# Attention value sums: the base block chosen for each half of the key rows, the rest of the window as 256-column products

## The reference

```python
q = apply_rope(...).reshape(B, nblk, WINDOW, KV_HEADS, Q_PER_KV, HEAD_DIM)   # 16 blocks of 128 queries
logits = jnp.einsum("bnqkgd,bnskd->bnkgqs", q, k_band)                       # 256 keys: block before, own block
valid = (diff >= 0) & (diff < WINDOW)                                        # diff = 128 + query - key
probs = softmax(concat([masked logits, sink]))[..., :-1]
o = jnp.einsum("bnkgqs,bnskd->bnqkgd", probs, v_band)
```

## Time and profile before

| | |
|---|---|
| median of three runs | 2229.74 us |
| span of the profiled execution | 2230.9 us |
| TensorE busy | 2163.5 us (97%) |
| VectorE, ScalarE, GpSimd busy | 64%, 46%, 46% |
| DMA share by slices | 44% to 99% |

### The profile page before, as it was taken

How to read it: one execution, slowest core, us unless ns; L and a number is a source line. 1 busy time by engine, 2 the same in 40 slices (tenths; PEclk the granted TensorE clock), 3 DMA queues, 4 the chain that set the end, 5 groups by cost and what they waited for, 6 DMA issues and landing times.

```text
span 2230.9 us, 28791 instructions
## 1 busy us (share of the span) xinstructions
PE 2163.5 (97%) x10410; PEld 1808.6 (81%) x10410; DVE 1436.8 (64%) x1815; ACT 1032.7 (46%) x1898; POOL 1037.3 (46%) x636
## 2 busy tenths in 40 slices
PE   5999999999999999999999999999999999999998
PEld 4887778788888878888787888887888888888887
DVE  6966548757476864554974653867676657657764
ACT  4334445634545644445644445434444434434442
POOL 2556775845553865544684555440222232232222
PEclk9999999999999999999999999999999999999999
DMA  9888899785559795557876565989677797787554
GB/s 344 307 300 309 310 319 343 236 309 174 201 189 334 277 322 173 197 192 279 312 277 247 179 211 206 353 341 361 226 282 243 260 342 251 268 313 274 196 203 170
DMA packets 244782, 592.86 MB, mean 266 GB/s; under 512 B 20928, under 2 KB 96800, under 8 KB 244256
## 3 DMA queue, kind: packets, MB, share of 16 engines
q1 hardware_dynamic: 241680, 585.71, 72.8%
q10 hardware_dynamic: 2960, 5.30, 0.7%
HBM read 461.96 MB, written 119.54 MB: 261 GB/s over the span
## 4 chain that ended last, share of the span: by engine, by line
PE 74%; DMA 7%; POOL 6%; DVE 5%; ACT 3%; DVEq 2%; POOLq 1%; issue 1%; SPq 1%; ACTq 0%
PE ps L2272 22%; PE ps L2274 22%; PE ps L2273 22%; POOL w_lo L1110 3%; DMA w_raw<-in_a_w_in 2%; PE ps L2477 2%; POOL cbl L1129 1%; PE ps L2527 1%; PE ps L2526 1%; PE ps L2552 1%; DMA zo<-tt 1%; DVE yb L2018 1%; DMA w_raw<-a_weights_combined 1%; DMA r<-b_input 1%; ACT w_hi L1304 1%
## 5 line engine op out<-in xcount | busy, mean ns | idle before, releaser
L1110 POOL TENSOR_TENSOR w_lo<-w_raw,w_hi 128x1024 fp32r<-128x1024 f32 x244 | 650.4, 2684 | 568.8 <-ACT w_hi L1304 568.8
L1304 ACT ACTIVATE w_hi<-w_raw 128x1024 fp32r<-128x1024 f32 x260 | 271.7, 1057 | 413.8 <-DMA w_raw<-in_a_w_in 370.2
L2272 PE MATMUL ps<-h,w_hi 128*128 128x512 f32 x1024 | 403.2, 394 | 10.2 <-POOL w_lo L1110 9.4
L2274 PE MATMUL ps<-h,w_lo 128*128 128x512 f32 x1024 | 398.9, 390 | 0.0
L2273 PE MATMUL ps<-h,w_hi 128*128 128x512 f32 x1024 | 398.7, 389 | 0.0
L1249 POOL TENSOR_SCALAR_AFFINE_SELECT pt<-pt 128x512 fp32r<-128x512 f32 x128 | 82.2, 642 | 395.4 <-ACT pt L1666 338.9
L2272 PEld LDWEIGHTS ps<-h,w_hi 128*128 128x128 f32 x1024 | 192.2, 188 | 55.5 <-POOL w_lo L1110 14.7
L2274 PEld LDWEIGHTS ps<-h,w_lo 128*128 128x128 f32 x1024 | 192.2, 188 | 40.6
L2273 PEld LDWEIGHTS ps<-h,w_hi 128*128 128x128 f32 x1024 | 192.4, 188 | 38.9 <-issue 0.2
L2272 PE MATMUL ps<-r,w_hi 128*128 128x512 f32 x480 | 191.7, 399 | 3.8 <-ACT kvf L1608 2.3
L2274 PE MATMUL ps<-r,w_lo 128*128 128x512 f32 x480 | 187.7, 391 | 0.0
(11 more groups left out here) (268 smaller groups left out, 4636.8 us busy)
## 6 DMA issues: line engine op xcount, KB each, us to landing
w_raw<-in_a_w_in SPq DMA_DIRECT2D x256, 256.0 KB, 3.6
w_hi<-b_weights_split SPq DMA_DIRECT2D x104, 512.0 KB, 4.4
w_lo<-b_weights_split SPq DMA_DIRECT2D x104, 512.0 KB, 5.8
w_raw<-in_a_w_in SPq DMA_DIRECT2D x52, 512.0 KB, 4.9
w_raw<-in_a_w_out SPq DMA_DIRECT2D x48, 512.0 KB, 5.7
w_hi<-v_weights_combined SPq DMA_DIRECT2D x48, 512.0 KB, 4.0
w_lo<-v_weights_combined SPq DMA_DIRECT2D x48, 512.0 KB, 5.1
w_hi<-a_weights_combined SPq DMA_DIRECT2D x32, 512.0 KB, 6.3
```

The costliest lines, as they stand in the source:

```text
L1110: g.tensor_tensor(wlo[p][:, rows_], raw[p][:, rows_], whi[p][:, rows_].bitcast(F32), ALU.subtract).then_inc(w_lo, 1)
L1304: s_.activation(whi[p][:, rows_], raw[p][:, rows_], ACT.Copy).then_inc(w_hi, 1)
L2272: t_.matmul(dst_, stat[0], mov[0], start=start, stop=False)
L2274: return t_.matmul(dst_, stat[1], mov[0], start=False, stop=stop)
```

## The change

The base block is chosen for each half of the key rows. Rows 0 to 63 take V of the own block, rows 64 to 127 take V of the block before (`vst` keeps no fifth block for that). What is then wrong are two corners: key rows 0 to 63 for queries 0 to 63 above the diagonal, and key rows 64 to 127 for queries 64 to 127 under it. Elsewhere a query half needs no correction in one half of the rows. So 64 rows are free in each correction, and the rest part of the probabilities is put there: one tile `pe_` of 128 rows holds the rounded part in one half and the rest in the other, with the difference of V (`edge_low`, `edge_up`) stored in both halves of the rows. Two corrections of 512 columns become two of 256.

With this go:

- TensorE: `values` issues two matmuls of 512 columns and two of 256, with separate waits ahead of them.
- VectorE: after L2234 two more subtractions of 64x256 that write the rests of the corners, before `pt_lo` is raised; L2234 itself raises the new `pt_all`. `kv_rest` has seven instructions for three, `kv_shift` two subtractions for one, and loses a copy.
- ScalarE: `kv_round` has seven instructions for three. The wait for `xk_out[1]` and `hb_out[1]` moves from the first write to `pt` to the first write to `pp`, since `pp` now lies on `hbs1`.
- GpSimd: `mask` has four selections of 64x256 for two of 128x512, a drain and a wait at its end.
- Some tiles move (`ot`, `obt`, the third `wh`), and `keep` with its two prologue instructions goes.

```diff
@@ places
-        pt = place("pt", v_at + 16 * K, [4, 512], F32R)
-        pp = place("pp", v_at + 24 * K, [2, 4, P + 1], F32)
+        pt = place("pt", v_at + 16 * K, [2, 512], F32R)
+        pp = place("pp", v_at + 20 * K, [2, 4, P + 1], F32)
+        edge_low = place("edge_low", v_at + 24 * K + 64, [NC, KVH, P], F32R)
+        pe_ = place("p_edge", v_at + 28 * K + 64, [2, 4 * HEAD], F32R)
@@ GpSimd, mask
-                for m, ready in ((0, pt_hi), (1, pt_lo)):
-                    pool.wait_ge(ready, a + 1)
-                    last = g.affine_select(out=pt[:, 2 + m].rearrange("p (h q) -> p h q", h=4),
...
+                pool.drain()
+                pool.wait_ge(pt_hi, a + 1)
+                kept(pe_[64:P, 1], high[64:P, :, HEAD:P], True)
+                kept(pe_[0:64, 0], high[0:64, :, 0:HEAD], False)
+                pool.wait_ge(pt_lo, a + 1)
+                kept(pe_[0:64, 1], pe_[0:64, 1].rearrange("p (h q) -> p h q", h=4), True)
+                kept(pe_[64:P, 0], pe_[64:P, 0].rearrange("p (h q) -> p h q", h=4), False).then_inc(pt_masked, 1)
+                pool.wait_ge(pt_masked, a + 1)
@@ ScalarE, kv_round
-                s_.activation(vst[:, 1:5, kh, 0:HEAD], kvf[:, 1:5, cols_], ACT.Copy)
-                s_.activation(dst[:, :, kh, 0:HEAD], df[:], ACT.Copy).then_inc(kv_hi_done, 1)
+                s_.activation(vst[0:64, :, kh, 0:HEAD], kvf[0:64, 1:5, cols_], ACT.Copy)
+                s_.activation(vst[64:P, :, kh, 0:HEAD], kvf[64:P, 0:4, cols_], ACT.Copy)
+                for there in (slice(0, 64), slice(64, P)):
+                    s_.activation(edge_low[there, :, kh, 0:HEAD], df[0:64], ACT.Copy)
+                    last = s_.activation(edge_up[there, :, kh, 0:HEAD], df[64:P], ACT.Copy)
+                last.then_inc(kv_hi_done, 1)
@@ ScalarE, attention steps
                     if a >= 2:
                         act.wait_ge(pv_full, a - 1)
-                    else:
-                        act.wait_ge(xk_out[1], 16 * 2)
-                        act.wait_ge(hb_out[1], 16 * 2)
                     s_.activation(pt[:, 0, :], bank(6), ACT.Copy).then_inc(pt_hi, 1)
                 if 0 <= a < ATT:
                     act.wait_ge(m_ready, a + 1)
                     if a >= 2:
                         act.wait_ge(pt_full, a - 1)
+                    elif a == 0:
+                        act.wait_ge(xk_out[1], 16 * 2)
+                        act.wait_ge(hb_out[1], 16 * 2)
@@ VectorE, kv_rest
-                v.tensor_tensor(vst[:, 1:5, kh, HEAD:P], kvf[:, 1:5, cols_], vst[:, 1:5, kh, 0:HEAD].bitcast(F32),
-                                ALU.subtract)
-                v.tensor_tensor(dst[:, :, kh, HEAD:P], df[:], dst[:, :, kh, 0:HEAD].bitcast(F32), ALU.subtract) \
-                    .then_inc(kv_lo_done, 1)
+                v.tensor_tensor(vst[0:64, :, kh, HEAD:P], kvf[0:64, 1:5, cols_], vst[0:64, :, kh, 0:HEAD].bitcast(F32),
+                                ALU.subtract)
+                v.tensor_tensor(vst[64:P, :, kh, HEAD:P], kvf[64:P, 0:4, cols_], vst[64:P, :, kh, 0:HEAD].bitcast(F32),
+                                ALU.subtract)
+                for there in (slice(0, 64), slice(64, P)):
+                    v.tensor_tensor(edge_low[there, :, kh, HEAD:P], df[0:64], edge_low[0:64, :, kh, 0:HEAD].bitcast(F32),
+                                    ALU.subtract)
+                    last = v.tensor_tensor(edge_up[there, :, kh, HEAD:P], df[64:P],
+                                           edge_up[64:P, :, kh, 0:HEAD].bitcast(F32), ALU.subtract)
+                last.then_inc(kv_lo_done, 1)
@@ VectorE, attention steps
-                    v.tensor_tensor(pt[:, 1, :], bank(6), pt[:, 0, :].bitcast(F32), ALU.subtract).then_inc(pt_lo, 1)
+                    v.tensor_tensor(pt[:, 1, :], bank(6), pt[:, 0, :].bitcast(F32), ALU.subtract).then_inc(pt_all, 1)
...
+                    v.tensor_tensor(pe_[64:P, 0].rearrange("p (h q) -> p h q", h=4), turned_p[0:64, :, 0:HEAD],
+                                    high[0:64, :, 0:HEAD], ALU.subtract)
+                    v.tensor_tensor(pe_[0:64, 1].rearrange("p (h q) -> p h q", h=4), turned_p[64:P, :, HEAD:P],
+                                    high[64:P, :, HEAD:P], ALU.subtract).then_inc(pt_lo, 1)
@@ TensorE, values
                 pe.wait_ge(kv_lo_done, at("kv_lo_done", g, kh + 1))
-                pe.wait_ge(pt_masked, a + 1)
                 if a >= 1:
                     pe.wait_ge(o_done, a)
+                pe.wait_ge(pt_hi, a + 1)
                 t_.matmul(bank(7), vst[:, blk, kh, :], pt[:, 0, :], start=True, stop=False)
+                pe.wait_ge(pt_all, a + 1)
                 t_.matmul(bank(7), vst[:, blk, kh, :], pt[:, 1, :], start=False, stop=False)
-                t_.matmul(bank(7), dst[:, blk, kh, :], pt[:, 2, :], start=False, stop=False)
-                t_.matmul(bank(7), dst[:, blk, kh, :], pt[:, 3, :], start=False, stop=True).then_inc(pv_full, 1)
+                pe.wait_ge(pt_masked, a + 1)
+                by_query = bank(7).rearrange("p (h q) -> p h q", h=4)
+                t_.matmul(by_query[:, :, 0:HEAD], edge_low[:, blk, kh, :], pe_[:, 0, :], start=False, stop=False)
+                t_.matmul(by_query[:, :, HEAD:P], edge_up[:, blk, kh, :], pe_[:, 1, :], start=False, stop=True) \
+                    .then_inc(pv_full, 1)
```

More of the change, by code:

```diff
@@ L442, in yoco_kernel @@
         zg = place("zg", v_at, [KT, T], F32)
-        pt = place("pt", v_at + 16 * K, [4, 512], F32R)
-        pp = place("pp", v_at + 24 * K, [2, 4, P + 1], F32)
+        pt = place("pt", v_at + 16 * K, [2, 512], F32R)
+        pp = place("pp", v_at + 20 * K, [2, 4, P + 1], F32)
+        edge_low = place("edge_low", v_at + 24 * K + 64, [NC, KVH, P], F32R)
+        pe_ = place("p_edge", v_at + 28 * K + 64, [2, 4 * HEAD], F32R)
+        obt = place("obt", v_at + 30 * K + 64, [2, P], F32)
         xs = place("xs", x_at, [NC, D], F32)
@@ L460, in yoco_kernel @@
         ks = place("ks", gt, [KVH, 2, 5 * P], F32R)
-        vst = place("vst", gt + 10 * K, [5, KVH, P], F32R)
-        ot = place("ot", gt + 15 * K, [2, P], F32)
+        vst = place("vst", gt + 10 * K, [NC, KVH, P], F32R)
         wst = place("wst", sp_at, [GROUPS, P], F32)
@@ L468, in yoco_kernel @@
         bsh = place("bsh", sp_at + 8 * K, [GROUPS * P], F32)
-        dst = place("dst", sp_at, [NC, KVH, P], F32R)
+        edge_up = place("edge_up", sp_at, [NC, KVH, P], F32R)
         kw = place("kw", sp_at + 4 * K, [T], F32)
@@ L472, in yoco_kernel @@
         df = place("df", sp_at + 11 * K, [NC, HEAD], F32)
-        obt = place("obt", v_at + 28 * K + 512, [2, P], F32)
         gb_at, wh_at = region(4 * K), region(4 * K)
@@ L477, in yoco_kernel @@
         gate_b = place("gate_b", gb_at, [D], F32)
-        wh = [place(f"wh{n}", w_at, [T], F32) for n, w_at in enumerate((wh_at, wh_at + 2 * K, v_at + 29 * K + 512))]
+        wh = [place(f"wh{n}", w_at, [T], F32) for n, w_at in enumerate((wh_at, wh_at + 2 * K, gt + 14 * K))]
         tt = [place(f"tt{n}", ga_at + 2 * K * n, [T], F32) for n in range(2)]
@@ L513, in yoco_kernel @@
         ident = place("ident", region(512), [P], F32)
-        ones = place("ones", region(512), [P], F32)
-        keep = place("keep", region(512), [P], F32)
+        ones_at = region(1024)
+        ones = place("ones", ones_at, [P], F32)
+        ot = place("ot", ones_at, [2, P], F32)
         prev = place("prev", region(512), [P], F32)
@@ L629, in yoco_kernel @@
         m_ready, r_ready, pt_lo, o_done = sem("m_ready"), sem("r_ready"), sem("pt_lo"), sem("o_done")
+        pt_all = sem("pt_all")
         zg_done, oz_lo = sem("zg_done", 8), sem("oz_lo", 8)
@@ L1088, in _ @@
             pool.drain()
-            g.affine_select(out=keep[:], in_=keep[:], compare_op=ALU.is_ge, fill=0.0, base=0,
-                            pattern=[[1, P]], channel_multiplier=-1)
             g.affine_select(out=prev[:], in_=prev[:], compare_op=ALU.is_gt, fill=0.0, base=0,
@@ L1237, in _ @@
                     g.memset(ks[:, :, :, 0:P].bitcast(F32), 0.0)
-                    g.memset(vst[:, 0].bitcast(F32), 0.0)
                     g.memset(kvf[:, 0, P:2 * P], 0.0).then_inc(zeroed, 1)
@@ L1245, in mask, with kept @@
             def mask(a):
-                for m, ready in ((0, pt_hi), (1, pt_lo)):
-                    pool.wait_ge(ready, a + 1)
-                    last = g.affine_select(out=pt[:, 2 + m].rearrange("p (h q) -> p h q", h=4),
-                                           in_=pt[:, m].rearrange("p (h q) -> p h q", h=4),
-                                           compare_op=ALU.is_ge, fill=0.0, base=0, pattern=[[0, 4], [1, P]],
-                                           channel_multiplier=-1)
-                last.then_inc(pt_masked, 1)
+                def kept(there, in_, low):
+                    heads = there.rearrange("p (h q) -> p h q", h=4)
+                    if low:
+                        return g.affine_select(out=heads, in_=in_, compare_op=ALU.is_ge, fill=0.0, base=0,
```

(10 more changed lines are left out.)

3 lines of the change are left out of this document (2 added, 1 removed).

## The result

The changed kernel took 2261.5 us (median of 4 runs, 2257.8 to 2265.1) against 2231.9 us for the kernel before in the same runs: ratio 1.0134, 95% interval [1.012, 1.0149], 30 us slower. A second series gave 1.0146 [1.0132, 1.016]. The forecast was 2243.2 us, slower by 0.6%; the time lies above its range. In what follows a ratio is turned into us with 2230: 1.0134 is +29.9.

What follows compares the result with a forecast made beforehand. TensorE's matmul stream was taken to bound the kernel. Terms: -14.4 (narrower matmuls) + 2.2 (lost savings) + 22 (late VectorE work) + 3.7 (moved wait) = 13.5 us, giving a median of 2243.2 us; range 2224 to 2253.

Steps and rivals of the forecast that it cites:

- windows 22: Groups of attention steps around `kv_rest` and `kv_round` where late VectorE work reaches TensorE: 22 us lost, bounds 8 and 25.
- savings lost in them 2.2: TensorE's matmul savings since each late VectorE chain began, lost at its wait: ten times 0.226, 2.2 us.
- the vanished gap -3.1: At `values(1)`, TensorE's old 3.1 us wait for VectorE, held by a rope transfer, was expected to go.
- +1.5 - 1.6: Low clock near the first attention steps: 1.5 us added behind the moved wait's new gap, the old gap's slow stretch removed.
- rival 4: Low clock after gaps over 3 us at steps 11, 28 and 46, some 1.5 us each: 2248 us; chance 0.15.
- TensorE's gain, 14.4: Two of four value matmuls halved in each of 64 steps, 0.226 us a step: 14.4 us saved, bounds 0 and 14.4.
- Rival 3: A 256-column value matmul with split output takes 0.233 us, so the gain is gone: 2257 us; chance 0.05.
- GpSimd's selections at nothing: GpSimd's four mask selections per step are not what comes last before the value matmuls, so they cost nothing.
- The gated output as what comes last: `values(a-1)` waits last for VectorE's `gated_output(a-2)`, not the mask; usually 2.1 us of slack, little where VectorE is behind.
- Rivals 1 and 2: First: VectorE idle time closes the windows, 2229.2 us, chance 0.16. Second: added VectorE work never adds up, 2222.5 us, 0.14.
- Two instructions, 0.84 a step: Two added VectorE subtractions between L2234 and the gated output, 0.42 us each, delay it by 0.84 us in all 64 steps.
- The moved wait, 3.7 within 0 and 9: ScalarE's wait ahead of the first exponentials delays `logits(1)` and `p_transposes(0)`: net 3.7 us lost, bounds 0 and 9.

Runs made afterwards that it cites:

- b_half: Kernel before with only the third and fourth value matmuls of each step cut to 256 columns, half the masked product left out: 2218.3 us, ratio 0.9952.
- d_masks: Kernel before with the narrower value matmuls and the changed kernel's form of the GpSimd masks, half the masked product left out: ratio 0.9955.
- c_mask: Changed kernel with GpSimd's masks reading the rest tile and moving the halves themselves, VectorE's two subtractions kept but unread: 2262.8 us, ratio 1.0144.
- a_gated: Changed kernel with VectorE's gated output of step a-2 placed ahead of the rests of step a-1: 2266.1 us, ratio 1.0157.
- b_edge: Kernel before with only the two added VectorE subtractions per step, written to a tile nobody reads: 2248.2 us, ratio 1.0088.
- b_kv: Kernel before with only the longer rounding and rests of keys and values (more instructions, not the changed kernel's order): 2237.7 us, ratio 1.0037.
- b_one: Kernel before with one unread added VectorE subtraction per step instead of two: 2237.1 us, ratio 1.0032.
- e_kv: Kernel before with the longer rounding and rests in the changed kernel's order, `df` in halves, no last value block copy: 2242.6 us, ratio 1.0055.

## Why the prediction was wrong

Split the forecast's sum into TensorE's idle and busy time, and the failed step stands out. Idle: windows 22, savings lost in them 2.2, the moved wait's gaps 6.9, the vanished gap -3.1: +28.0 us. The trace has +28.6 (+25.2 in the second profile). Busy: -14.4 for the matmuls, +1.5 for one new stretch of low clock, -1.6 for the old one: -14.5. The trace has -0.4 (+1.9 in the second). **The whole error of some 16 us (in busy time 14.1 in the first profile, 16.4 in the second) is matmul time behind the new gaps, nearly all of it at low clock.** The step that failed is the term for it, +1.5 - 1.6, next to nothing: I had priced it for one new gap. The mechanism was in rival 4, which gave it to three gaps of more than 3 us and 4.5 us in all. It came in seven stretches, most of them behind waits of 1.7 to 2.7 us. It took 11 us by the mean granted clock, 13.7 in the attention part alone, 14 by the busy time (in which the last matmul ahead of each gap also counts in full, 0.39 us, where 0.23 is the distance to the next).

That the sum of idle time came out within 0.6 us is in part luck. Up to `values(2)` the trace has 2.7 us more of it, where I had 6.9 - 3.1 = 3.8; my windows have 23.3 more, where I had 22 + 2.2; three waits for copies that I left out add 3.8, and other waits went or got shorter, by some 2 us.

Point by point:
- *TensorE's gain, 14.4*: right (14.6 in b_half's busy time). Rival 3 falls.
- *GpSimd's selections at nothing*: right (d_masks, c_mask).
- *The gated output as what comes last*: right in the profile, and too narrow. a_gated shows that the masks stand next to it. b_edge shows what the late VectorE delays besides: ScalarE's copies of keys and values, which stand behind the exponentials in its queue. I left these out at three places, 1633.67, 1828.77 and 2022.48. This is the second: VectorE's row maximum, behind late work, then ScalarE's exponentials and copies, then TensorE. The same wait is 1.16 us in the kernel before and in b_kv, 2.15 in b_one and 2.93 in b_edge, so it is the edges' two subtractions that lengthen it:

```profile
1823.57 1.28 DVE L2214 SCALAR_TENSOR_TENSOR x<-x,r,fn 128x1024 f32<-128x1024 f32 x1 [0.86 <-POOL r L1283]
1824.77 0.44 DVE L2178 COPY kvf<-kvf 128x128 f32<-128x128 f32 x1
1825.12 0.68 DVE L2237 COPY_PREDICATED ps<-prev,ps 128x512 f32<-128x512 uint32 x1
```

```profile
1826.85 0.37 ACT L1683 ACTIVATE pp<-ps,negm 128x129 f32<-128x129 f32 x1 [2.90 <-DVE negm L2247]
...
1828.23 1.21 ACT L1615 ACTIVATE kvf<-ps 128x256 f32<-128x256 f32 x4
```

```profile
1828.77 0.47 PE L2295 MATMUL ps<-r,w_hi 128*128 128x512 f32 x1 [2.59 <-ACT kvf L1615]
```

- *The windows, 22*: the sum of idle time was right, its places in part. From the value sums' starts, kernel after less kernel before, low clock included: steps 3 and 4 lose 2.4 us (forecast 1.8), 11 and 12 5.4 (3.5), 19 and 20 3.1 (2.3), 28 to 30 3.5 (4.9), 35 4.4 (3.55), 46 and 47 5.0 (3.2), 51 to 53 4.4 (2.0). Rivals 1 and 2 fall: nothing closed again.
- *Two instructions, 0.84 a step*: a little more, 1.0. The gated output used to begin 0.59 us behind the rest, and begins 1.60 us behind it now (rest to edge 0.71, 0.44, edge to gated output 0.45). VectorE got 79 us busier, where I had said 68. `kv_rest` +1.85: 1.9 measured; `kv_round` +1.7: 1.8.
- *The moved wait, 3.7 within 0 and 9*: 5.1 alone, 5.6 when taken back. Its mechanism is as told: the exponentials sit behind the store, the gap of step 1 is gone. The split between idle time and clock is not: two gaps of 3.79 and 1.87 us less the 1.21 that stood there before are 4.5 us where I had 6.9, and the low clock behind them took 5.2 where I had 1.5. Not foreseen either: the table load of 1.28 us, which ran at 1531.02 in the kernel before and now stands behind the wait, and the store, which landed 8.5 us after its issue instead of 10.7.
- *VectorE and GpSimd in each other's way*: the one instruction of a unit of rests that meets a normalisation still takes the time that it took before; the units with one are 0.6 to 0.8 us longer than the others (3.9 to 4.0 us against 3.2 to 3.4), as before (2.2 against 1.3 to 1.5). That the two exclude each other, as the Trainium skill has it (SBUF — State Buffer, "Who interferes with whom"), the trace bears out; that four more exposed instructions lose more, it doesn't, since one of them or three are over in the time of the same one normalisation.
- *The range*: its upper end, 2253, is 2 us above what its own terms give (2243.2 + 3 + 5).

## What to carry to other kernels

Price a gap on a TensorE that is otherwise always busy with a chance of more than its length: here 28 us of new idle time brought 11 to 14 us of slow matmuls with it, and much of both went when the gaps were taken away. It doesn't always come: e_kv has 7.9 us of new idle time in waits up to 2.7 us, and its mean granted clock is 0.999. A saving on the bounding engine that is bought with instructions on a 64% busy one has to be checked at each place where that engine's queue is behind, for everyone whom it serves, not only for the consumer of the new result. Work moved to an engine and slot with real slack (here GpSimd's existing masks, and a later slot) kept the saving.

## What the runs showed of the hardware

The length of a gap doesn't decide alone whether the clock falls: TensorE's waits of 1.71 us at 1617.13 and 2.69 at 1925.39 were followed by granted clocks of 0.50 to 0.62, those of 2.54 at 1868.35 and 2.58 at 2022.48 by 1.00. Nor does the program alone: in the second profile of the changed kernel the same wait at `values(29)` was as long and the clock fell.

```profile
1866.81 0.51 PE L2584 MATMUL ps<-pt,vst 128*128 128x512 f32 x1 [2.54 <-issue]
...
1867.00:1869.00 2.00, 2.00 (x7) 1.66 (x7) 1.78 (x4) 0.87 (x2) 0.67 (x1) 0.52 0.87 215
```

What does decide stays open. And instructions of 64 rows and 256 columns have two prices on VectorE and ScalarE, 0.34 and 0.31 us from start to start on the same half of the rows (b_kv), 0.43 where each works on the other half than the last (kernel after); in eight units of six such instructions that is 7 us of engine time, and the runs that differ by it, with small other edits, differ by 4 and 6 us, with intervals that overlap.
